# Recurrent mixing on TensorE: chunk matrices as stacked 64x64 blocks instead of full 128x128 ones

## What is computed

```python
def step(state, inp):
    r_t, w_t, k_t, v_t, na_t, b_t = inp
    sa = jnp.einsum('bhvk,bhk->bhv', state, na_t)
    state = state * w_t[:, :, None, :] + sa[..., None] * b_t[:, :, None, :] + v_t[..., None] * k_t[:, :, None, :]
    return state, jnp.einsum('bhvk,bhk->bhv', state, r_t)
```

## Time and profile before

| | us |
|---|---|
| median of 3 runs | 1924.41 |
| lowest and highest | 1921.27, 1924.89 |
| span of the profiled execution, first to last instruction | 1917.9 |
| of it, the mixing stage, from the first gram to the last `values` | 251.0 (196.79 to 447.80) |
| TensorE busy in the span | 1824.5 (95%) |
| mean granted TensorE clock | 0.985 |

### The profile page before, as it was taken

The page is one execution under the profiler, slowest core; times in us unless marked ns, Lnnn a source line. Parts: engine busy times, 40 slices in busy tenths (PEclk is TensorE's granted clock), DMA queues, the critical chain, the costliest instruction groups (busy, mean ns, idle before and its releaser), DMA issues.

```text
span 1917.9 us, 32920 instructions
## 1 busy us (share of the span) xinstructions
PE 1824.5 (95%) x10454; PEld 1615.6 (84%) x10454; DVE 1449.1 (76%) x2932; ACT 734.0 (38%) x1320; POOL 587.2 (31%) x446
## 2 busy tenths in 40 slices
PE   3999899999789999999999999999999999999996
PEld 2776788885379999999999999999988888888885
DVE  6886556564837887858888889867688888888887
ACT  3342433450244545553333333332433333333331
POOL 5023422230043535353323233245233223332310
PEclk8999999999999999999999999999999999999998
DMA  8841000004524334358888998899899999999981
GB/s 297 290 128 33 1 1 1 2 1 165 189 88 129 119 118 132 130 206 272 293 296 298 312 306 290 291 328 387 349 409 373 351 354 353 355 355 356 353 291 70
DMA packets 245051, 435.06 MB, mean 227 GB/s; under 512 B 84898, under 2 KB 157956, under 8 KB 244996
## 3 DMA queue, kind: packets, MB, share of 16 engines
q1 hardware_dynamic: 207968, 300.07, 45.3%
q0 software_dynamic: 36864, 134.23, 19.0%
q10 hardware_dynamic: 164, 0.05, 0.0%
HBM read 379.77 MB, written 54.53 MB: 226 GB/s over the span
## 4 chain that ended last, share of the span: by engine, by line
PE 71%; DVE 1%; ACT 0%; issue 0%; ACTq 0%; DVEq 0%
PE bank L1585 28%; PE bank L1993 9%; PE bank L1992 9%; PE bank L1994 9%; PE bank L1565 6%; PE bank L1929 5%; PE bank L1975 4%; PE bank L1941 1%; DVE n_stats L1341 0%; DVE wide L2305 0%; DVE wide L2303 0%; DVE wide L1350 0%; PE bank L1934 0%; DVE wide L1355 0%; ACT uh L1593 0%
## 5 line engine op out<-in xcount | busy, mean ns | idle before, releaser
L1585 PE MATMUL bank<-hh,uh 128*128 128x384 f32 x1024 | 357.1, 349 | 0.0
L1585 PE MATMUL bank<-hl,uh 128*128 128x384 f32 x1024 | 343.0, 335 | 0.0
L1992 PE MATMUL bank<-vh,wh 128*128 128x512 f32 x768 | 299.4, 390 | 3.1 <-DVE wl L2264 3.1
L1994 PE MATMUL bank<-vh,wl 128*128 128x512 f32 x768 | 299.5, 390 | 0.0
L1993 PE MATMUL bank<-vl,wh 128*128 128x512 f32 x768 | 299.4, 390 | 0.0
L1643 POOL DMA_INDIRECT vsel<-in_peer_v,picks x128 | 149.6, 1169 | 416.4 <-DVE gt L1669 401.8
L2097 ACT ACTIVATE vh<-vraw 128x1024 fp32r<-128x1024 f32 x128 | 135.9, 1062 | 287.1 <-PE bank L1994 271.0
L1643 POOL DMA_INDIRECT wide<-in_peer_u,picks x108 | 148.0, 1371 | 231.1 <-DVE wide L1650 217.8
L2261 DVE TENSOR_TENSOR vl<-vraw,vh 128x1024 fp32r<-128x1024 f32 x128 | 156.6, 1224 | 81.3 <-ACT vh L2097 81.3
L1585 PE MATMUL bank<-hh,ul 128*128 128x384 f32 x1024 | 198.9, 335 | 0.0
L1585 PEld LDWEIGHTS bank<-hl,uh 128*128 128x128 f32 x1024 | 192.9, 188 | 0.0
(11 more groups left out here) (342 smaller groups left out, 3199.6 us busy)
## 6 DMA issues: line engine op xcount, KB each, us to landing
urows<-in_peer_u SPq DMA_DIRECT2D x128, 512.0 KB, 8.1
vraw<-in_peer_v SPq DMA_DIRECT2D x128, 512.0 KB, 6.1
scored<-act_out SPq DMA_DIRECT2D x128, 192.0 KB, 3.4
gates<-SS SPq DMA_DIRECT2D x16, 1536.0 KB, 13.9
gtile<-gates SPq DMA_DIRECT2D x32, 768.0 KB, 7.4
act_in<-scored SPq DMA_DIRECT2D x128, 192.0 KB, 6.2
wt<-in_w_in SPq DMA_DIRECT2D x19, 512.0 KB, 4.7
wq<-in_peer_wq SPq DMA_DIRECT2D x18, 512.0 KB, 3.8
```

The lines of the kernel that those rows point to most:

```text
L1585: last = pe.matmul(bank, u[:, k, :], h[:, k, 0:TD], start=(n == 0), stop=(n == 3 * KD - 1))
L1992: pe.matmul(b, wh[s][:, cols], vh[s][:, half], start=first, stop=False)
L1994: last = pe.matmul(b, wl[s][:, cols], vh[s][:, half], start=False, stop=stop)
```

## The change

- BM, KM, DT, DD, XX, NL, GT, HS, dPL and S keep only the blocks: [128, heads, 64], with the first chunk's (or first head's) 64x64 block on partitions 0 to 63 and the second's on 64 to 127. The masks and the identity are folded the same way (`eye`, and two additions on GpSimd in the setup).
- Each 128x128 product over tokens becomes two 64x64 products (`blocks`): one with weights and moving rows on partitions 0 to 63 and its output on 0 to 63 of the bank, one with 64 to 127 for all three. They are issued in turn, so that they stand in opposite corners of the array. Grams, qt, g, h, y, st and S x QT are split alike, by chunk and head.
- DD of the next level is no longer a transpose of DT: it is a third product, DT x XX, issued ahead of the product that gives the new DT (`ev["d"]` before `ev["t"]`); the first DD is DT x eye.
- Copies and masks on VectorE, ScalarE and GpSimd are [128, 4, 64] where they were [128, 4, 128]. Masks are two instructions of four heads instead of four of two. The products with `diag2` go; BH and KH are one copy instead of two. QT and Y are written in two halves, Y from banks 4 and 2, and TensorE waits for its own event `yq` ahead of S x QT.

```diff
             step(pool.memset(window[:, :, :], 0.0))
 
...
+            pool.tensor_tensor(eye[:, :], ident[:, 0:CH], ident[:, CH:], ALU.add)
...
-        BM, KM = (sb(n, [P, HEADS, 2, P]) for n in ("BM", "KM"))
+        BH, KH = (sb(n, [P, 4, P]) for n in ("BH", "KH"))
+        BM, KM = (sb(n, [P, HEADS, 2, CH]) for n in ("BM", "KM"))
         PT = sb("PT", [P, HEADS, 2, P])
-        NL = [[PT[:, 4 * g + 2 * b:4 * g + 2 * b + 2, :, :].rearrange("p a b c -> p (a b) c") for b in range(2)]
...
-        DD, DT, XX = ([sb(f"{n}{g}", [P, 4, P]) for g in range(2)] for n in ("DD", "DT", "XX"))
+        DD, DT, XX = ([sb(f"{n}{g}", [P, 4, CH]) for g in range(2)] for n in ("DD", "DT", "XX"))
         WW = sb("WW", [P, 2, HEADS, HD])
...
-        dPL = sb("dPL", [P, 2, 4, P])
-        S = [sb(f"S{c}", [P, 4, P]) for c in range(2)]
...
+        def half(c):
+            return slice(CH * c, CH * c + CH)
...
-                halves(BH, 6, "trB")
-
-            def halves(dst, b, name):
-                for c in range(2):
-                    act.activation(dst[:, c, :, :], four(banks[b][:, :]), ACT.Copy,
-                                   scale=diag2[:, CH * c:CH * c + 1]).then_inc(ev[name], 1)
+                act.activation(BH[:, :, :], four(banks[6][:, :]), ACT.Copy).then_inc(ev["trB"], 1)
...
                     for g in range(2):
+                        if l < LV - 1:
+                            now("d", 2 * (l - 1) + g + 1)
+                            act.activation(DD[g][:, :, :], four(banks[2 + g][:, 0:4 * CH]), ACT.Copy)\
+                                .then_inc(ev["dc"], 1)
                         now("t", 2 * (l - 1) + g + 1)
-                        act.activation(DT[g][:, :, :], four(banks[6 + g][:, :]), ACT.Copy).then_inc(ev["tc"], 1)
-                    for g in range(2 if l < LV - 1 else 0):
-                        now("d", 2 * (l - 1) + g + 1)
-                        act.activation(DD[g][:, :, :], four(banks[2 + g][:, :]), ACT.Copy).then_inc(ev["dc"], 1)
+                        act.activation(DT[g][:, :, :], four(banks[6 + g][:, 0:4 * CH]), ACT.Copy)\
+                            .then_inc(ev["tc"], 1)
...
         def _(pe):
-            def grams(src, n, first, name):
-                for e in range(2):
-                    for j in range(2):
-                        p = 2 * (first // 2) + j
-                        rows = slice(64 * e, 64 * e + 64)
-                        last = pe.matmul(banks[(0 if name == "gramB" else 2) + first + e][:, 256 * j:256 * j + 256],
-                                         src[rows, p, cols(n)], PK[rows, p:p + 5:4, cols(n)], start=True, stop=True)
-                    last.then_inc(ev[name], 1)
+            def grams(src, n, b, name):
+                for p in range(4):
+                    for c in range(2):
+                        for e in range(2):
+                            ins = pe.matmul(banks[b + e][half(c), P * p:P * p + P], src[half(e), p, cols_half(n, c)],
+                                            PK[half(e), p:p + 5:4, cols_half(n, c)], start=True, stop=True)
+                            if p == 3 and c == 1:
+                                ins.then_inc(ev[name], 1)
...
+            def blocks(b, width, left, right):
+
+                for i in range(4):
+                    for c in range(2):
+                        last = pe.matmul(banks[b][half(c), i * width:(i + 1) * width], left[half(c), i, :],
+                                         right(i)[half(c)], start=True, stop=True)
+                return last
...
                     variances(n - 1)
                 for g in range(2):
                     now("dt0", g + 1)
-                    for h in range(4):
-                        last = pe.transpose(banks[g][:, h * P:(h + 1) * P], DT[g][:, h, :], ident[:, :])
-                    last.then_inc(ev["dd0"], 1)
...
-                        for h in range(4):
-                            last = pe.matmul(banks[6 + g][:, h * P:(h + 1) * P], XX[g][:, h, :],
-                                             DT[g][:, h, :], start=True, stop=True)
-                        last.then_inc(ev["t"], 1)
-                    if l < LV - 1:
-                        for g in range(2):
-                            now("tc", 2 * (l - 1) + g + 1)
-                            for h in range(4):
-                                last = pe.transpose(banks[2 + g][:, h * P:(h + 1) * P], DT[g][:, h, :], ident[:, :])
-                            last.then_inc(ev["d"], 1)
+                        if l < LV - 1:
+                            blocks(2 + g, CH, DT[g], lambda i: XX[g][:, i, :]).then_inc(ev["d"], 1)
+                        blocks(6 + g, CH, XX[g], lambda i: DT[g][:, i, :]).then_inc(ev["t"], 1)
...
+                    for c in range(2):
+                        last = pe.matmul(banks[4][half(c), h * HD:(h + 1) * HD], KM[half(c), slot(h), 0, :],
+                                         VT[half(c), h * HD:(h + 1) * HD], start=True, stop=True)
...
-                    for h in range(4):
-                        last = pe.matmul(banks[g][:, h * P:(h + 1) * P], DT[g][:, h, :],
-                                         RH[:, :, 4 * g + h, :], start=True, stop=True)
-                    last.then_inc(ev["w"], 1)
+                    blocks(g, P, DT[g], lambda i: RH[:, :, 2 * i + g, :]).then_inc(ev["w"], 1)
...
+                def heads_out(bank, c, left, right):
+                    for p in range(4):
+                        for e in range(2):
+                            last = pe.matmul(banks[bank][half(e), p * CH:(p + 1) * CH], left(2 * p + e),
+                                             right(2 * p + e), start=True, stop=True)
+                    return last
...
+                for c in range(2):
+                    heads_out(c, c, lambda h: WW[half(c), 0, h, :], lambda h: BM[half(c), slot(h), 1, :])\
+                        .then_inc(ev["qt"], 1)
                 for c in range(2):
                     now("ptc", c + 1)
-                    for p in range(4):
-                        last = pe.matmul(banks[2 + c][:, p * P:(p + 1) * P], WW[:, 0, 2 * p:2 * p + 2, :],
-                                         BH[:, c, p, :], start=True, stop=True)
-                    last.then_inc(ev["g"], 1)
+                    heads_out(2 + c, c, lambda h: WW[half(c), 0, h, :], lambda h: lanes(c, h)).then_inc(ev["g"], 1)
...
                     for p in range(4):
-                        pe.matmul(banks[6 + c][:, p * P:(p + 1) * P], BH[:, c, p, :],
-                                  WW[:, 1, 2 * p:2 * p + 2, :], start=True, stop=False)
-                        last = pe.matmul(banks[6 + c][:, p * P:(p + 1) * P], KH[:, c, p, :],
-                                         VT[:, p * P:(p + 1) * P], start=False, stop=True)
+                        for u in range(2):
+                            for e in range(2):
+                                h = 2 * p + e
+                                left = lanes(c, h) if u == 0 else KH[half(c), p, half(e)]
+                                right = WW[half(c), 1, h, :] if u == 0 else VT[half(c), h * HD:(h + 1) * HD]
+                                last = pe.matmul(banks[6 + c][half(e), p * CH:(p + 1) * CH], left, right,
+                                                 start=(u == 0 and p == 0), stop=False, skip_group_check=True)
                     last.then_inc(ev["h"], 1)
...
+                        for u in range(2):
+                            for e in range(2):
+                                h = 2 * p + e
+                                left = WW[half(c), 1, h, :] if u == 0 else VT[half(c), h * HD:(h + 1) * HD]
+                                last = pe.matmul(banks[Y_BANK[c]][half(e), p * CH:(p + 1) * CH], left,
+                                                 (BM, KM)[u][half(c), slot(h), 1, :], start=(u == 0 and p == 0),
+                                                 stop=False, skip_group_check=True)
+                last.then_inc(ev["yq"], 1)
+                now("qtc", 2)
                 pe.wait_ge(ev["ready"], START + 1)
+
+                now("yq")
...
                     for p in range(4):
-                        o = banks[4][:, p * P + CH * c:p * P + CH * c + CH]
-                        last = pe.matmul(o, S[c][:, p, :], QT[:, p, CH * c:CH * c + CH], start=False, stop=True,
-                                         skip_group_check=True)
-                    if c == 1:
-                        last.then_inc(ev["y"], 1)
+                        for e in range(2):
+                            last = pe.matmul(banks[Y_BANK[c]][half(e), p * CH:(p + 1) * CH], S[c][half(e), p, :],
+                                             QT[half(e), p, half(c)], start=False, stop=True, skip_group_check=True)
...
-                        for e in range(2):
-                            mask(n, 4 + e, KM, "maskK", 1, e)
-                    elif l <= 3:
+                    if 2 <= l <= 3:
...
```

(81 more changed lines are left out.)

78 lines of the change are left out of this document (41 added, 37 removed).

## The result

The changed kernel takes 1846.67 us (median of 4 runs, 1843.13 to 1848.84), the kernel before 1923.72 on the same chip. The ratio is 0.960, 95% interval 0.9592 to 0.9616: 77 us faster, where 64 was forecast (1860, inside the range 1840 to 1922).

What follows compares the result with a forecast made beforehand. TensorE, busy 95% of the span, was taken as the bound. Savings of 16.5 us per tile, 66 over four, less 0.5 for `w_out`, gave span 1852.4; adding 6.5 gave 1859, taken as 1860, range 1840 to 1922.

Steps and rivals of the forecast that it cites:

- The price of a pair: Two 64x64 products in opposite corners of TensorE: 0.12 us taken, between bounds of 0.12 and 0.255.
- Both halvings: Full product's 0.24 us halved for the columns, and two products side by side: 0.12 per pair.
- rival 1: Corners sharing a PSUM bank don't overlap: 14 us per tile lost of the 16.5 gain, 1914 us; chance 0.13.
- Rival 2: TensorE records fed too slowly, 32 ns each, 0.255 us per pair: 18 us slower, 1942; chance 0.12 in full.
- Rival 3: Clock falls; all mixing at 1.2 GHz would be 69 us slower, 1993; chance 0.05 for half or more.
- Levels 2 to 5: Mixing tile's levels: 6.34 to 4.45, 5.27 to 3.2, 6.65 to 5.0, 3.69 to 2.2 us.
- level 4's wait for VectorE: In level 4, VectorE's about 5 us of work exceeds TensorE's 3.2: 1.8 us late, stretch 5.0.
- The beginning: Tile start to end of first scores: 18.28 to 13.0 us, with shorter masks and DT operations; gain 5.3.
- ScalarE ahead of W: Before W, ScalarE's exponentials and DT and RH copies run late: wait 1.8 us, stretch 5.55 to 6.5, loss 0.95.
- qt, g, h and y: Late tile stretches: qt, g, h 6.51 to 3.9 us as 32 pairs; y 3.32 to 2.3 with a wait.
- The end: Before the output rows, `w_out`'s transfer may be late: 0.5 us taken, 0 to 3.
- The four tiles: Mixing stage: 16.5 of 62.9 us saved per tile, 46.4 left; 66 us over four tiles.

Runs made afterwards that it cites:

- experiment 5: Changed kernel with every product of `blocks` (dd0, xx, d, t, W) issued twice: 1897.33 us, ratio 0.9873 to the kernel before.
- experiment 1: Changed kernel with each block's four products on partitions 0 to 63 issued first, then the four on 64 to 127: 1859.61 us, ratio 0.9676 to the kernel before.
- experiment 4: Changed kernel with VectorE's XX addition done twice in a row: 1853.24 us, ratio 0.9645 to the kernel before.
- experiment 7: Changed kernel with GpSimd's dPL and decayed keys after the last XX product, attention output scaled before the first mask, six `w_out` transfers earlier: 1838.30 us.

## Why the prediction was right

- **The price of a pair.** 0.12 taken, 0.117 measured, and experiment 5 shows that pairing is two thirds of the gain (12.4 of 19.3 us a tile). Both halvings hold: experiment 1 has a product alone in its corner at 0.117, half of the full 0.24, and a second corner beside it adds nothing. The first was less sure than the text made it, since the x0 row, with 64 moving columns in the full array, cost 0.22. The rule of the Trainium skill (TensorEngine Tiling (Array Packing), "Gotcha 1: PSUM Pressure") that different row tiles cannot access one PSUM bank simultaneously did not show in the time: `blocks` writes one bank from both row halves, on different partitions, and pairs fully. That is rival 1 (the prediction's text, where it names the rule, calls it the second), and it is out. Its price was put at 14 us a tile with x0, S and st in it; experiment 5, without these, has 12.4.
- **Rival 2** is out: records follow each other every 15 ns (32 in 0.47 us), half of the 29 from which it decided.
- **Rival 3** is out for the tiles, 1.00 in the last three as before. That it can happen in this kernel is seen in experiment 4, where one of the tiles two to four had a fall after its longer waits.
- **Levels 2 to 5** came within 0.25 us each, the wait of 0.3 between xx and d included, and level 4's wait for VectorE was in the forecast: 1.8 more than level 3, measured 1.64 (4.77 less 3.13). The beginning, 12.6 for 13.0: one DT multiplication was 0.76 (0.75 taken).
- **The term that was mis-sized: ScalarE ahead of W.** A wait of 1.8 was forecast, 0.44 came. Timeline of ScalarE in the third tile:

```profile
311.16 0.50 ACT L955 ACTIVATE SC<-SC,nm 128x256 f32<-128x256 f32 x1
...
314.21 0.63 ACT L982 ACTIVATE DT<-bank 128x256 f32<-128x256 f32 x2
314.74 0.58 ACT L990 ACTIVATE RH<-bank 128x512 f32<-128x512 f32 x1
```

  The six exponentials take 3.05 us, not the 3.57 that a window with a copy in it had suggested, and the two DT copies 0.63 together, not 0.76; then RH's copy frees W at 315.37. The stretch is 1.0 us shorter than forecast, and not 1.4, as TensorE's own work in it is 5.0 and not 4.7.
- **Also mis-sized: qt, g, h and y**, 3.04 and 2.18 for 3.9 and 2.3. 64 products in 3.04 us are 0.095 per pair. Chunk 0 sits on one row half and chunk 1 on the other, in different banks, and g of chunk 0 starts at 318.88, among qt of chunk 1, whose last record starts at 319.05. More than two corners are then at work. The grams, which alternate between all four, show it at its most: 16 products of 128 columns in 1.04 us (285.88 to 286.92), 0.065 each. W's, of the same width in two corners, are 16 in 1.90 (315.37 to 317.27), 0.119 each. Together 1.0 us per tile.
- **The end.** `w_out` late by 0.5 was forecast. Its packets ended at 376.2 here by the slices of the DMA view, and the stretch is 0.9 longer. In the six profiles of small blocks with the transfers at their old place the output rows start about 0.53 us after the last packet (here 376.22 and 376.75), and in experiment 7, with earlier transfers, the delay is gone: this is the cause.
- **Not in the sum: what the clock gives and takes elsewhere.** The setup's instructions are the same but for three small ones of GpSimd, yet it took 2.2 us longer. Windows from 0 to the start of the stage, of the kernel before, the changed one and experiment 7:

```profile
0.00:196.79 196.79, 158.92 (x657) 119.77 (x658) 140.81 (x180) 65.25 (x87) 54.68 (x71) 0.95 0.56 182
```

```profile
0.00:198.96 198.96, 161.29 (x657) 120.99 (x658) 141.45 (x180) 65.52 (x87) 56.62 (x74) 0.93 0.55 180
```

```profile
0.00:195.93 195.93, 158.53 (x657) 119.53 (x658) 141.39 (x180) 65.44 (x87) 56.59 (x74) 0.97 0.56 183
```

  The length follows the mean clock, 0.97, 0.95, 0.93, over kernels with the same setup, and the other small-block runs have 197.0 to 199.2, so it is no effect of the change. (Experiment 1's profile gives 197.9 at 0.99, but its first clock record stands only at 52 us.) The 2.4 us lost behind the stage may have the same cause (mean clock 0.89 against 0.92 in the 108.4 us after the output rows begin), but this was not tested, and it may not be chance alone: from the output rows to the end the two kernels with full products take 1466.3 and 1466.5, the seven with small blocks 1467.3 to 1469.9.
- **Not in the sum: the profile of before was a fast one.** The forecast added 6.5, the distance of the median from the profiled span. For the changed kernel that distance is 1.2, and its profiled run took 1.75 more than its own span. By that, as an estimate, the profiled execution of before took about 1919.7, under all its measured runs (1921.27 and more). So the median gained 77.1 where the two spans differ by 72.4, and 5.3 of the forecast's error is this term.

The errors add up. The four tiles gave 78.0 for the 66 forecast, 12.0 more. The late `w_out` took 0.4 more than forecast, the setup 2.2, and what follows the stage 2.4. That leaves 7 us of span; with the 5.3 above and the 1 us of rounding up it makes the 13.3 by which 1846.7 lies under 1860. The tiles were put too slow in nearly every stretch. The mechanism was right; the sizes were cautious.

## What to carry to other kernels

Where a float32 product is half zeros, cutting it into 64x64 blocks in opposite array corners halves its TensorE time: here 0.117 us for the two products that replace one of 0.24. Issue them alternately between the corners (0.467 us a block here, 0.575 with the halves in turn), and keep several corners busy across loops too. Then look for what the shorter TensorE time uncovers, copies of 0.4 us, small VectorE operations beside GpSimd, a weight transfer that had slack, and move those; a rearrangement that removes a wait but adds products paid here only once the products were small.

## What the hardware did that I had not expected

- TensorE starts float32 records 15 ns apart on average. It takes them out of list order between corners, but only a product or two ahead: a half block of four products began 0.29 us after the one before it, not together with it (experiment 1). Four corners at once run grams of 128 columns in 0.065 us each.
- A VectorE operation on four elements per partition took 0.98 us (from 307.32) beside a GpSimd operation of 1.05 (from 307.22), and 0.17 without.
- The setup of the same code took 195.9 to 199.2 us from run to run, with mean clock 0.97 to 0.93.
